# Four levels of a triangular inverse on TensorE: one loop of four passes, or four copies in a row

## The chip, the cores and the metric

The kernel runs on one core of a Trainium2 chip. The metric is device time in microseconds (us), from launch to the last store, for one execution of the whole program. Lower is better.

## The reference

The program computes two transformer-like blocks on 256 tokens of width 1024. The first is a gated linear recurrence, sparse attention and a mixture of 32 experts. The second has a cross attention, a convolution, a bidirectional RWKV-7 recurrence and a feed-forward stage of 16 experts with three weight matrices each. The change lies in the RWKV-7 recurrence of the second block:

```python
def wkv7_scan(r, w, k, v, kk, a, reverse):
    def step(state, inp):
        r_t, w_t, k_t, v_t, kk_t, a_t = inp
        sa = jnp.einsum('bhij,bhj->bhi', state, -kk_t)
        state = (state * w_t[..., None, :]
                 + sa[..., :, None] * (kk_t * a_t)[..., None, :]
                 + v_t[..., :, None] * k_t[..., None, :])
        y_t = jnp.einsum('bhij,bhj->bhi', state, r_t)
        return state, y_t
```

It has 6 heads of width 64 and runs once forward and once in reverse over the 256 tokens. After it come a projection (`w_out`), the router and the experts:

```python
hid = jax.nn.silu(jnp.einsum('becd,edf->becf', xe, w_gate)) * jnp.einsum('becd,edf->becf', xe, w_up)
ye = jnp.einsum('becf,efd->becd', hid, w_down) * gates[..., None].astype(h.dtype)
```

Everything is float32. The expert weights of the second block alone are 16 x 3 x 4 MB.

## The kernel before

All five engines run one instruction stream each. SyncE (`sp`) issues the weight loads, 2 MB each, into rings and free pieces of on-chip memory, in a fixed order, each after a wait on the semaphore that says that its place is free.

The recurrence is done in chunks of 32 tokens. The outer loop over `PAIRS` runs twice and is written out: in pair 0 the forward direction (`d` = 0) works on the first 128 tokens and the reverse direction (`d` = 1) on the second 128, in pair 1 they swap. Each pair has 4 chunks, 6 heads and 2 directions, so nearly every step is 48 small products, with operands of 32 or 64 partitions. `product` (L2317) issues all of them. The compiler makes two weight loads and two matmuls of one such float32 product, so the trace shows 96 matmuls for 48 products. In order, TensorE does for each pair:

- `turned`: transposes of three inputs of each direction;
- `pair_products`: the chunk products of both directions, 96 products in all;
- `bonus`: 48 products, then two waits on `prod_out` (L2477);
- the loop `with pe.Fori(0, 4) as lev` (L2478), a loop that the engine's sequencer runs with registers and a branch. Each pass inverts the unit triangle one level further (blocks of 1 to 2, ... up to 32 rows): `merge_first` (L2363) for both directions, 24 products each of `OM` and `X` into PSUM, then `merge_second` (L2374), 24 products each of `XT` and `PONE`. A pass is thus 96 products, 192 matmuls and 192 weight loads. The waits in it compare a semaphore with `lev * 2 + const` or `lev * 4 + const`, which the sequencer works out in registers;
- `solved`, `reads`: 48 products each, with the inverse;
- `additions`: 192 products, with `strips` put in between. A strip is one product of 128x128 that belongs to the output projection and is on no one's critical path. `STRIPS` says by hand where they go, counted in products from the start of a direction's additions: in pair 0 six at 34 and six at 92 of the first direction, and twelve at 48 of the second; in pair 1 at 27, 85 and 41;
- `advance`: four short sequential steps of the state, each with an answer from ScalarE in between, some strips beside them.

Beside each level the other engines work in turn: VectorE adds the identity to the first product (L3395), ScalarE copies the second (L1402), VectorE transposes that copy (L3399), GpSimd masks the next `OM` (L973). Their four levels are written out already.

In SyncE's order two loads belong to this stretch: one 2 MB piece of `w_e_down` (L709) goes when `lev_full` reaches 1, that is with the first `merge_first` of pair 0, and the next loads of expert weights (L704, four 2 MB pieces to begin with) wait for `y_out` to reach 4, which VectorE gives at the end of pair 1 (L3429). The memory that they fill is in use by the recurrence until then.

Of the kernel before, what the change touches and what calls it, by code (L numbers as in the profile page):

```python
# [137 lines left out]
def build(nc, A, out):  # L138
    with ExitStack() as ctx:
# [5 lines left out]
        def S(name):  # L145
            if name not in sems:
                sems[name] = ctx.enter_context(nc.semaphore(name))
            return sems[name]
# [1336 lines left out]
        def _(pe):  # L1485
# [833 lines left out]
            def turned(p, d):  # L2319

                pe.wait_ge(S("prep_ready"), 4 * p + 2 + d + 1)
                if p:
                    pe.wait_ge(S("y_out"), 2 * p - 1 + d)
                    pe.wait_ge(S("state_out"), 2 * NC4 * p - 1 + d)
                    pe.wait_ge(S("strips_out"), 2 * p - 1 + d)
                for b, src in ((2, KKIN), (3, PEND), (0, KEND)):
                    if not p:
                        is_out(pe, prior[4 * d + b])
                    for c in range(3):
                        ins = nc.tensor.transpose(dbank(d, b, c * P, P), src[d][:, c, :], ident)  # L2330
                    ins.then_inc(S("tok_full"), 1)

            def pair_products(p, d, i):

                if i == 0:
                    if not p:
                        is_out(pe, prior[4 * d + 1])
                    pe.wait_ge(S("tok_out"), 6 * p + 3 * d + 1)
                else:
                    pe.wait_ge(S("tok_out"), 6 * p + 3 * d + 3)  # L2340
                a = (PIN, KIN)[i][d]
                both = front[d][:, 0:1152].rearrange("p (w q) -> p w q", w=3)[:, 0:2 + p:1 + p]
                for pc in range(3):
                    for c in range(NC4):
                        tc = slice(32 * c, 32 * c + 32)
                        for par in range(2):
                            r = slice(64 * par, 64 * par + 64)
                            o = dbank(d, ((1, 2), (0, 3))[i][par], 0, 192)[tc].rearrange("p (w n) -> p w n", w=2)
                            ins = product(o[:, :, 32 * pc:32 * pc + 32], a[r, pc, tc],
                                          both[r, :, P * pc + 32 * c:P * pc + 32 * c + 32])  # L2350
                ins.then_inc(S("prod_full"), 1)

            def bonus(p, d, t):

                pe.wait_ge(S("prod_out"), 8 * p + 2 + 2 * d + 2)
                for h in range(HEADS6):
                    for c in range(NC4):
                        tc = slice(32 * c, 32 * c + 32)
                        ins = product(dbank(d, 0, 64 * h, 64)[tc], block32(BT[d], c, unit(h)),
                                      VTOK[tc, t, 64 * h:64 * h + 64])  # L2360
                ins.then_inc(S("rhs_full"), 1)

            def merge_first(p, d, lev):  # L2363

                pe.wait_ge(S("om_out"), lev * 2 + (14 * p + 4 + d + 1))
                pe.wait_ge(S("x_out"), lev * 2 + (10 * p + d + 1))
                pe.sem_inc(S("level_begun"), 1)
                for u in range(HEADS6):
                    for c in range(NC4):
                        ins = product(dbank(d, 3, 32 * u, 32)[32 * c:32 * c + 32], block32(OM[d], c, u),  # L2370
                                      block32(X[d], c, u))
                ins.then_inc(S("lev_full"), 1)

            def merge_second(p, d, lev):  # L2374

                pe.wait_ge(S("lev_out"), lev * 4 + (16 * p + d + 1))
                pe.sem_inc(S("level_begun"), 1)
                for u in range(HEADS6):
                    for c in range(NC4):
                        ins = product(dbank(d, 3, 192 + 32 * u, 32)[32 * c:32 * c + 32], block32(XT[d], c, u),  # L2380
                                      block32(PONE[d], c, u))
                ins.then_inc(S("lev_full"), 1)

            def solved(p, d):

                pe.wait_ge(S("lev_out"), 16 * p + 14 + d + 1)
                pe.wait_ge(S("solve_out"), 6 * p + d + 1)
                pe.wait_ge(S("prod_out"), 8 * p + 6 + d + 1)
                for i in range(2):
                    for h in range(3 * i, 3 * i + 3):  # L2390
                        for c in range(NC4):
                            tc = slice(32 * c, 32 * c + 32)
                            ins = product(dbank(d, 1 + i, 128 * (h - 3 * i), 128)[tc], block32(XT[d], c, unit(h)),
                                          RHS[d][tc, h, :])
                    ins.then_inc(S("rhs_full"), 1)
# [4 lines left out]
            def reads(p, d):  # L2400

                pe.wait_ge(S("solve_out"), 6 * p + 2 + 2 * d + 2)
                for h in range(HEADS6):
                    for c in range(NC4):
                        tc = slice(32 * c, 32 * c + 32)
                        ins = product(lane(d, c, h, 0, 96), WU[d][tc, h, 0:64], PP[d][tc, h, :])
                ins.then_inc(S("qg_full"), 1)
# [7 lines left out]
            def strip(p, k, s):  # L2415
                product(ps[:, 512 * s:512 * s + P], MIX[:, k, p * P:(p + 1) * P],
                        wout2[s // 4][:, k, s % 4 * P:s % 4 * P + P], False)
# [10 lines left out]
            def additions(p, d, t):  # L2428

                pe.wait_ge(S("rg_out"), 4 * p + 2 * d + 2)  # L2430
                for i in range(2):
                    for h in range(HEADS6):
                        for c in range(NC4):
                            tc, hc = slice(32 * c, 32 * c + 32), slice(64 * h, 64 * h + 64)
                            a, b = (PTOK[d][tc, h, :], WU[d][tc, h, 64:128]) if i == 0 else \
                                (KTOK[d][tc, hc], VTOK[tc, t, hc])
                            strips(p, d, 24 * i + 4 * h + c)
                            ins = product(lane(d, c, h, 192, 64), a, b, i == 0 and h < 2)
                for i in range(2):
                    for h in range(HEADS6):  # L2440
                        for c in range(NC4):
                            tc, hc = slice(32 * c, 32 * c + 32), slice(64 * h, 64 * h + 64)
                            a, b = (WU[d][tc, h, 64:128], PR_[d][tc, h, :]) if i == 0 else \
                                (VTOK[tc, t, hc], block32(KR[d], c, unit(h)))
                            strips(p, d, 48 + 24 * i + 4 * h + c)
                            ins = product(lane(d, c, h, 384, 32), a, b, False)
                if not p:
                    ins.then_inc(S("step_full"), 1)
# [19 lines left out]
            for p, pair in enumerate(PAIRS):  # L2468
                for d, t in pair:
                    turned(p, d)  # L2470
                for i in range(2):
                    for d, t in pair:
                        pair_products(p, d, i)
                for d, t in pair:
                    bonus(p, d, t)
                for d, t in pair:
                    pe.wait_ge(S("prod_out"), 8 * p + 2 + 2 * d + 2)  # L2477
                with pe.Fori(0, 4) as lev:  # L2478
                    for d, t in pair:
                        merge_first(p, d, lev)  # L2480
                    for d, t in pair:
                        merge_second(p, d, lev)
                for d, t in pair:
                    solved(p, d)
                for d, t in pair:
                    reads(p, d)
                for d, t in pair:
                    additions(p, d, t)
                assert not units[p]
                for s in range(-1, NC4):  # L2490
                    for d, t in pair:
                        if s >= 0:
                            advance(p, d, s)
                        for b in STEP_STRIPS.get((p, s, d), ()):
                            strip(p, 3, b)
# [1085 lines left out]
```

## Time and profile before

| | us |
|---|---|
| median of 3 runs | 1618.83 (1616.43 to 1620.4) |
| the profiled execution's own time | 1615.83 |
| its span, first to last instruction | 1614.0 |
| TensorE busy | 1319.3 (82%), mean granted clock 0.91 |
| VectorE, ScalarE, GpSimd busy | 457.7, 284.1, 132.4 |
| DMA | 514 MB, mean 318 GB/s |
| recurrence of the second block | about 1041 to 1135 of the span |

How to read it: the share of the chain of waits is PE 52% and DMA 42%, and the two take turns. In the stages of the experts (530 to 910 and 1200 to 1600 in the span) the DMA engines move 428 GB/s without a gap. In between TensorE leads, and in the recurrence the DMA engines are almost idle (3 to 97 GB/s in these slices of the page). Times of rows are microseconds from the start of the span. [...]

### The profile page before, as it was taken

How to read it: one execution, taken by the hardware profiler on the slowest of the kernel's cores; microseconds unless marked ns; L12 is line 12 of the kernel's file. 1: busy time of each engine (PE TensorE's matmuls, PEld its weight loads, DVE VectorE, ACT ScalarE, POOL GpSimd, SP SyncE). 2: the span in 40 equal slices, each digit the busy share in tenths (PEclk: the TensorE clock that was granted, in tenths of full speed). 3: DMA queues.
4: the chain of work that ended last, by engine and by line, in shares of the span. 5: the costliest groups of instructions: out<-in, count | busy, mean ns of one | idle time of the engine just before them, and what ended most of it. 6: DMA issues, size and time to landing. Idle time of an engine off the chain costs nothing.

```text
span 1614.0 us, 27193 instructions
## 1 busy us (share of the span) xinstructions
PE 1319.3 (82%) x11722; PEld 745.9 (46%) x11722; DVE 457.7 (28%) x968; ACT 284.1 (18%) x634; POOL 132.4 (8%) x289
## 2 busy tenths in 40 slices
PE   5999999999999887787778689988886657666665
PEld 4765887888563332232223278677432212211211
DVE  1346337431463322222222243753510000000001
ACT  0101214650021110111011113332211101101001
POOL 4000013000000000000000004122000000000000
PEclk9999999999999989988999889998998787888878
DMA  9799665133479999999999691310899999999997
GB/s 346 280 389 340 189 235 178 65 108 133 158 277 421 428 427 428 429 428 428 428 428 426 289 339 54 97 56 3 358 426 427 427 428 428 428 428 429 428 427 295
DMA packets 86630, 513.98 MB, mean 318 GB/s; under 512 B 8537, under 2 KB 13066, under 8 KB 61842
## 3 DMA queue, kind: packets, MB, share of 16 engines
q1 hardware_dynamic: 82450, 502.84, 76.7%
q0 software_dynamic: 3424, 9.27, 1.6%
q8 instruction: 66, 1.08, 0.3%
q10 hardware_dynamic: 672, 0.65, 0.1%
q14 instruction: 18, 0.15, 0.0%
HBM read 507.84 MB, written 3.15 MB: 317 GB/s over the span
## 4 chain that ended last, share of the span: by engine, by line
PE 52%; DMA 42%; DVE 2%; issue 1%; ACT 1%; SPq 1%; POOL 0%; DVEq 0%; ACTq 0%
PE ps L1518 42%; DMA arena<-in_w_e_down 19%; DMA ring<-in_exp_w 19%; PE ps L2317 4%; DMA ring<-in_w_e_up 2%; PE ps L1610 2%; DMA ring<-in_w_in 1%; PE ps L2089 1%; PE ps L2567 0%; PE ps L1766 0%; SPq L653 0%; PE ps L1762 0%; PE ps L1565 0%; PE ps L2330 0%; PE ps L2118 0%
## 5 line engine op out<-in xcount | busy, mean ns | idle before, releaser
L1518 PE MATMUL ps<-ring,arena 128*32 128x512 f32 (+4 forms) x1844 | 268.1, 650 | 101.1 <-DMA ring<-in_exp_w 85.3
L1518 PE MATMUL ps<-ring,hTs 128*32 128x512 f32 (+2 forms) x992 | 214.7, 633 | 46.1 <-DMA ring<-in_w_e_up 25.0
L1518 PE MATMUL ps<-hTs,ring 128*128 128x256 f32 (+1 forms) x992 | 215.5, 381 | 0.0
L1518 PEld LDWEIGHTS ps<-ring,arena 128*32 128x32 f32 (+1 forms) x1844 | 81.8, 128 | 267.5 <-issue 178.9
L1518 PEld LDWEIGHTS ps<-hTs,ring 128*128 128x128 f32 (+1 forms) x992 | 182.9, 188 | 29.1 <-issue 4.5
L1518 PE MATMUL ps<-arena,vv 128*32 128x512 f32 (+2 forms) x560 | 92.1, 710 | 84.5 <-DMA arena<-in_w_e_down 78.0
L1518 PEld LDWEIGHTS ps<-ring,hTs 128*32 128x32 f32 (+1 forms) x992 | 76.1, 136 | 155.0 <-issue 106.4
L3142 DVE COPY hTs<-ps 64x512 f32<-64x512 f32 x32 | 22.2, 693 | 259.5 <-PE ps L1518 259.5
L1518 PE MATMUL ps<-arena,hTs 128*32 128x512 f32 x480 | 95.0, 632 | 0.0
L1518 PEld LDWEIGHTS ps<-arena,vv 128*32 128x32 f32 (+2 forms) x560 | 28.1, 142 | 132.4 <-DMA arena<-in_w_e_down 86.3
L1236 ACT COPY arena<-ps 128x512 f32<-128x512 f32 x32 | 18.7, 585 | 387.9 <-PE ps L2067 387.9
L1518 PE MATMUL ps<-arena,ring 128*128 128x256 f32 (+2 forms) x320 | 69.7, 382 | 2.8 <-issue 2.0
L3523 DVE TENSOR_TENSOR vv<-vv,ps 64x512 f32<-64x512 f32 x16 | 11.0, 690 | 212.4 <-ACT vv L1465 212.4
L1518 PEld LDWEIGHTS ps<-arena,ring 128*128 128x128 f32 (+1 forms) x320 | 59.0, 190 | 13.3 <-issue 5.7
L2089 PE MATMUL ps<-arena 64*128 64x512 f32 x256 | 63.0, 610 | 1.6 <-DVE arena L3151 1.6
L3517 DVE TENSOR_TENSOR hTs<-ps,nffn 128x128 f32<-128x128 f32 x32 | 7.8, 285 | 194.8 <-PE ps L1518 194.8
L900 POOL COPY arena<-arena 128x128 f32 (+1 forms) x64 | 16.9, 293 | 437.9 <-PE ps L2067 417.0
L1465 ACT ACTIVATE vv<-ps 64x512 f32<-64x512 f32 x16 | 9.4, 590 | 207.6 <-PE ps L1518 207.6
L1518 PEld LDWEIGHTS ps<-cst,low 64*128 64x128 f32 (+1 forms) x544 | 33.1, 189 | 27.4 <-issue 27.4
L1518 PE MATMUL ps<-arena 128*32 128x512 f32 (+7 forms) x270 | 44.5, 409 | 0.0
L2823 DVE SCALAR_TENSOR_TENSOR arena<-ring,ccol,arena 128x512 f32<-128x512 f32 x56 | 42.1, 752 | 2.0
L1471 ACT COPY hTs<-ps 128x512 f32<-128x512 f32 x16 | 9.4, 585 | 163.1 <-PE ps L1518 163.1
(473 smaller groups left out, 1470.9 us busy)
## 6 DMA issues: line engine op xcount, KB each, us to landing
ring<-in_exp_w SPq DMA_DIRECT2D x91, 2048.0 KB, 21.8
arena<-in_w_e_down SPq DMA_DIRECT2D x28, 2048.0 KB, 25.7
ring<-in_w_e_gate SPq DMA_DIRECT2D x24, 2048.0 KB, 32.1
ring<-in_w_e_up SPq DMA_DIRECT2D x24, 2048.0 KB, 37.7
ring<-in_w_in SPq DMA_DIRECT2D x22, 2048.0 KB, 13.7
ring<-in_ada_w SPq DMA_DIRECT2D x12, 2048.0 KB, 15.9
arena<-in_w_e_up SPq DMA_DIRECT2D x8, 2048.0 KB, 34.7
arena<-in_w_e_gate SPq DMA_DIRECT2D x8, 2048.0 KB, 33.2
```

Of the source, the lines that this page charges most:

```text
L900: ins = nc.gpsimd.tensor_copy(gateR[:, t], mid(gatep1[:, t, cols], 4))
L1236: nc.scalar.copy(HT1, ps[:, m * 512:m * 512 + 512]).then_inc(S("hidT1_ready"), 1)
L1465: nc.scalar.activation(hid2, u[0:64], ACT.Silu).then_inc(S("silu2_ready"), 1)
L1471: nc.scalar.copy(YE, ps[:, 1024:1536]).then_inc(S("ye_ready"), 1)
L1518: return nc.tensor.matmul(o, lhsT, rhs, start=start, stop=stop)
L1610: ins = nc.tensor.matmul(o, wt[:, k, c * P:(c + 1) * P], hT[:, k, :], start=k == 0 and c % 2 == 0, stop=k == KC - 1, skip_group_check=True)
L2089: ins = nc.tensor.matmul(ps[:, b * 512:b * 512 + 512], HT1[r, 256 + t * P:256 + (t + 1) * P], YE1[r, :], start=False, stop=True, skip_grou ...
L2317: return nc.tensor.matmul(o, lhsT, rhs, start=start, stop=True, skip_group_check=True)
L2823: ins = stt(part, wt[:, k, :], ccol[:, k:k + 1], part, ALU.mult, ALU.add)
L3142: cp(part1, u[64:128]).then_inc(S("part_ready"), 1)
L3517: ins = tt(xe[:, ks], v3(ps[:, o:o + P], 4), last(nffn8[:, ks], CAP), ALU.mult)
L3523: tt(hid2, hid2, ps[64:128, (e % 2) * 512:(e % 2) * 512 + 512], ALU.mult).then_inc(S("hid2_ready"), 1)
```

## The change

TensorE's loop over the four levels becomes a loop of Python, so that its body stands four times in the instruction stream. It does so in both pairs. The products, their order and the work of the other engines stay. `lev` is then a number: the waits compare with constants, and the register operations, the compare and the branch are gone.

```diff
@@ -2475,7 +2475,7 @@
                     bonus(p, d, t)
                 for d, t in pair:
                     pe.wait_ge(S("prod_out"), 8 * p + 2 + 2 * d + 2)
-                with pe.Fori(0, 4) as lev:
+                for lev in range(4):
                     for d, t in pair:
                         merge_first(p, d, lev)
                     for d, t in pair:
```

## Rows read from the trace of the kernel before

**Rows 1.** The page, part 3: DMA queue, packets, MB, share of 16 engines.

```profile
q8 instruction: 66, 1.08, 0.3%
```

**Rows 2.** Timeline of TensorE, pair 0: start, length, operation, count, idle before.

```profile
1048.66 0.75 PE L2317 MATMUL ps<-arena,ring 32*32 32x64 f32 x36 [1.22 <-issue]
1049.47 1.20 PE L2317 MATMUL ps<-ring 32*32 32x32 f32 x88
1053.09 1.76 PE L2317 MATMUL ps<-ring 32*32 32x32 f32 x104 [2.42 <-issue]
1055.17 3.05 PE L2317 MATMUL ps<-ring 32*32 32x32 f32 x192 [0.31 <-issue]
1058.52 2.58 PE L2317 MATMUL ps<-ring 32*32 32x32 f32 x192 [0.30 <-issue]
1061.53 2.42 PE L2317 MATMUL ps<-ring 32*32 32x32 f32 x192 [0.43 <-ACT ring L1402]
1064.21 1.51 PE L2317 MATMUL ps<-arena,ring 32*32 32x128 f32 x48 [0.25 <-DVE ring L3399]
...
1069.36 0.72 PE L2317 MATMUL ps<-ring,arena 32*64 32x64 f32 x42 [0.83 <-DVE ring L3406]
```

**Rows 3.** The same timeline for pair 1.

```profile
1095.30 0.87 PE L2317 MATMUL ps<-arena,ring 32*32 32x64 f32 x48 [1.61 <-issue]
1096.26 1.29 PE L2317 MATMUL ps<-ring 32*32 32x32 f32 x76
1098.82 1.94 PE L2317 MATMUL ps<-ring 32*32 32x32 f32 x116 [1.27 <-issue]
1101.13 3.05 PE L2317 MATMUL ps<-ring 32*32 32x32 f32 x192 [0.37 <-ACT ring L1402]
1104.47 2.91 PE L2317 MATMUL ps<-ring 32*32 32x32 f32 x192 [0.29 <-issue]
1107.81 2.42 PE L2317 MATMUL ps<-ring 32*32 32x32 f32 x192 [0.43 <-ACT ring L1402]
1110.46 1.51 PE L2317 MATMUL ps<-arena,ring 32*32 32x128 f32 x48 [0.23 <-DVE ring L3399]
```

**Rows 4.** DMA queues in the window 1065 to 1083, after the loop of pair 0.

```profile
q8 instruction: 6, 0.10, 2.1%
```

**Rows 5.** DMA queues in 1055.1 to 1064.2, passes 2 to 4 of pair 0.

```profile
q8 instruction: 1, 0.02, 0.7%
```

**Rows 6.** DMA queues in 1101.1 to 1110.4, passes 2 to 4 of pair 1; all rows.

```profile
q14 instruction: 1, 0.01, 0.3%
```

**Rows 7.** Line 2478, the loop's own instructions: count, ns min/median/max, first and last start.

```profile
L2478 PEldq FUSED_REGOPS  x8: 50/50/50, 1049.2 to 1107.5; - x8
...
L2478 PEldq COMPARE_BRANCH  x8: 76/220/246, 1054.6 to 1110.1; - x8
```

**Rows 8.** Timeline of SyncE, the weight loads around the stretch.

```profile
1050.18 0.33 SPq L709 DMA_DIRECT2D arena<-in_w_e_down  x1
1135.10 0.33 SPq L704 DMA_DIRECT2D ring<-in_w_e_up  x1
```

**Rows 9.** Waits of SyncE from 1041 to 1170: waiter, releaser, us, times, longest.

```profile
SPq L704 <- DVE arena L3429: 84.5, 1, 84.5
```

**Rows 10.** Busy time by engine in four stretches; then PEclk, DMA share, GB/s.

```profile
1055.10:1058.20 3.10, 3.03 (x192) 2.95 (x192) 1.42 (x4) 0.45 (x2) 1.18 (x2) 0.50 0.57 238
...
1061.50:1064.20 2.70, 2.38 (x192) 2.11 (x192) 1.46 (x4) 0.52 (x2) 2.70 (x3) 1.00 0.00 0
...
1134.50:1170.00 35.50, 28.85 (x116) 14.48 (x116) 20.48 (x53) 8.87 (x15) 3.95 (x4) 0.90 0.97 404
...
1204.00:1590.00 386.00, 252.93 (x1806) 81.65 (x1798) 15.79 (x41) 33.65 (x55) 10.85 (x40) 0.82 1.01 428
```

**Rows 11.** Timeline of TensorE, one group of six strips in pair 0.

```profile
1073.11 1.60 PE L2317 MATMUL ps<-ring,hTs 128*128 128x128 f32 x12
```

**Rows 12.** Chain of waits, its first long DMA piece after the recurrence.

```profile
1204.96 22.54 DMA arena<-in_w_e_down
```

## The prediction

> **What bounds the kernel now.** I read the page first. The chain of waits alternates between TensorE and DMA, so the stage has to be found in which the change lies. It is the recurrence, 1041 to 1135. There SyncE waits 84.5 us for one thing, the last result of pair 1 [rows 9], and issues the next expert weights the moment it has it, at 1135.10 [rows 8]. From then on the DMA engines are full (share 0.97 at 404 GB/s, later 1.01 at 428) [rows 10], and from 1204.96 the chain is mostly DMA [rows 12]. So what the recurrence gains or loses moves the start of a full stream of loads and reaches the end one for one. Nothing absorbs it: the loads that could run early are held back by memory, not by time.
>
> Next I read the timeline of TensorE in this stretch, looking at what stands in the brackets. A pass of the loop is 192 matmuls. Passes 2, 3 and 4 of pair 0 start at 1055.17, 1058.52 and 1061.53, and the code behind the loop at 1064.21 [rows 2]: 3.35, 3.01 and 2.68 us. The short waits between them, 0.25 to 0.43 us, are answers of ScalarE and VectorE or the loop's own instructions. But pass 1 starts at 1049.47 and takes 5.7 us, for it stands still for 2.42 us after 88 matmuls, put down to "issue". In pair 1 pass 1 stops for 1.27 us after 76 matmuls, and a stop of 1.61 us lies just ahead of it, in `bonus` [rows 3]. In the middle of a row of like products no semaphore can be meant.
>
> The queues explain it. Instructions come by DMA, 66 packets and 1.08 MB, so 16.4 KB each [rows 1]. From the restart at 1095.30 to the one at 1098.82 there are 48 + 76 = 124 matmuls and as many weight loads, with 8 or so instructions of the sequencer: 256, or 64 bytes each. At 1048.66 and 1053.09 it is 36 + 88 = 124 again. One packet thus holds 256 instructions, and **TensorE stops at the end of a packet until the next is there**. In code that runs straight the packets follow at 3.52 us (1095.30 to 1098.82), and six of them lie within 18 us, at most 3.6 us apart [rows 4]. In passes 2 to 4 pair 0 has one packet in 9.1 us and pair 1 has none of this queue [rows 5, 6]: these passes run out of instructions that are there already. That is the point of the case. 192 matmuls and 192 loads are 1.5 packets; fetched, they cost 5.3 us, and from the loop 2.7 to 3.35.
>
> **The change part by part.** *Taken away:* in each of two pairs 3 taken branches, their register work and that of the waits. The branch takes 220 ns and the register operation 50 [rows 7]. The idle time ahead of the passes bounds what this can give, 0.29 to 0.43 us at a time, six times: 2.0 us at most if the code were there for nothing. As part of it is an answer of ScalarE, I would take half, but in fetched code it hides behind the fetch, so 0 goes into the sum.
>
> *Added:* three copies of a pass for each pair, 384 instructions and about 4 waits each, 1164; the loop's own in the one pass that stays, some 10, go. 1154 / 256 = 4.5 packets a pair. The price of a packet is the nearest row's, 3.5 us, since these passes are the same products as the ones that were stopped. 4.5 x 3.5 = 15.8 us a pair.
>
> *Replaced:* what TensorE did from the restart in pass 1 to the end of the loop. Pair 0: 1053.09 to 1064.21 is 11.1 us, of which one packet's 3.5 would pass anyway, so 7.6 go. Pair 1: 1098.82 to 1110.46 is 11.6, so 8.1 go. Net: 15.8 - 7.6 = **8.2** and 15.8 - 8.1 = **7.7 us**, together 15.9.
>
> Is the rest of a pass a stronger limit than the fetch? At the lower clock a pass is 3.05 us [rows 2, 10] plus 0.3 us of waiting, that is 2.2 us for each packet's worth. It is under 3.5, so answers and clock both hide behind the fetch inside the levels, and ScalarE, VectorE and GpSimd only wait longer.
>
> *A load beside it:* one 2 MB load goes out at 1050.18 [rows 8], and the restart that should come 3.5 us after 1048.66 comes after 4.43 [rows 2]. That load is still running at 1055 to 1058 (share 0.57) [rows 10], where the changed kernel fetches its second packet. I take the same 0.9 us again. Bounds: 0 and 1.8.
>
> *The strips:* a group of six takes 1.60 us [rows 11] and gives the fetch time. Pair 0 is moved by half a packet (4.5), so the groups stand elsewhere among the packets: the twelve strips of direction 1 fall into a packet with about 52 products of 2 short matmuls (some 12 ns each), 3.2 + 1.2 = 4.4 us, while their neighbours still take 3.5. Against an even spread that is 0.9 to 1.7 us; I take 1.3, bounds 0 and 2. In pair 1 the shift is 9.0 packets in all, so nothing changes there. The wait of 0.83 us for VectorE at 1069.36 [rows 2] now overlaps with a fetch: -0.5, bounds -0.8 and 0.
>
> *The clock:* in the loops the granted clock is at 0.50 for some passes and back at 1.00 in the last one of pair 0 [rows 10]. [...] The dense work of the loop is what stood ahead of the rise before. I take 0, bounds 0 and 4 for both pairs.
>
> Sum: 15.9 + 0.9 + 1.3 - 0.5 = **17.6 us**. On the profiled execution, 1615.83, that is 1633.4. Its own time is 3.0 us under the median of the runs, and on the median it is 1618.8 + 17.6 = **1636.4**.
>
> [...]
>
> **The rivals.**
> *The copies come for nothing (faster).* If the fetch ran on ahead while TensorE waits for ScalarE and VectorE in each level, only the loop's own cost would go: six times about 0.3 us, 1618.8 - 1.9 = 1616.9. It decides from the point at which a packet comes in less than the 2.0 us that its share of a pass takes. For it: before the stops there is always work without answers to wait for. Against it: six packets in 18 us also hold in `additions` and `advance`, where answers are waited for. [...]
>
> *The fetch is hidden in part.* If waiting time lets the next packet be asked for early, a packet would cost about 2.6 us instead of 3.5: 9 x 0.9 = 8.1 less, 1628. Same evidence against it.
>
> *The stops feed on each other.* The clock stays at the lower level after both pairs (+4) and each packet costs what the one at 1053.09 did for half of them (+0.9 x 4): 1644.
>
> *It doesn't do what it says:* none of weight; both forms issue the same products.
>
> **How the numbers follow.** Forecast, the sum within its bounds: 0.78. Low end: 15.9 - 0.8 with a packet at 3.45 (9 x 0.05 less) and the second restart not late, 14.6, so 1633; high end: 15.9 + 1.8 + 2 + 4 = 23.7, so 1642.5. Stops that feed on each other: 0.08. Hidden in part: 0.08. For nothing: 0.06. To leave no more than 2 in 10 out I reach on the low side toward the partly hidden case and on the high side to the third rival: 1630 to 1644. A measurement of this kernel can tell about 0.3%, 4.9 us, from no change. Slower by more: 0.78 + 0.08 + 0.08 = 0.94 less a little, 0.93. Same: 0.05. Faster: 0.02, since the fast rival's 1.9 us lies within the 0.3%.
>
> **What would show it.** The changed trace should have about 75 packets in q8 instead of 66, nine of them where the levels run. Each level should take 5 to 5.7 us on TensorE with stops of 1 to 2 us at "issue" in the middle of its products, 128 matmuls apart at most. The first expert load should leave at about 1152.7 instead of 1135.10, and the DMA stage after it should be as long as before. Wrong would be: levels of 3 us; no more packets in q8; packets closer than 3 us; or a later stage that gives the time back.

## The result, and the profile after

| | us |
|---|---|
| before, median of 4 runs | 1618.68 (1616.43 to 1620.40) |
| after, median of 4 runs | 1643.85 (1640.88 to 1647.38) |
| ratio after to before | 1.0159, 95% interval 1.0145 to 1.0172 |
| the profiled execution of after | 1646.21, span 1644.4 |

The four levels written out are slower, by 25.2 us where 17.6 were forecast. The interval of the ratio is 23.5 to 27.8 us. The time lies at the very end of the stated range, 0.15 us inside it, and with the ratio taken on the median that was known then just outside it (1618.83 x 1.0159 = 1644.6). It is beyond the 1642.5 that the sum's own bounds allowed. Medians and ratios here leave out one disturbed run (`e7_load_in_steps`, 2171.9 us at a granted clock of 0.55).

The page of the changed kernel has nine more packets in "q8 instruction" than [rows 1], as counted ahead, and "q14 instruction" has 18 on both pages. Only TensorE's code differs, so q8 is the queue that brings it its instructions (packets, MB, share):

```profile
q8 instruction: 75, 1.23, 0.3%
```

The timeline of TensorE in pair 0, the rows that wait for "issue" and the first row of the additions, answers to [rows 2] (start, length, operation, count, idle before; where the bracket has "issue", the trace names no engine and no line that TensorE waited for):

```profile
1049.37 0.95 PE L2317 MATMUL ps<-arena,ring 32*32 32x64 f32 x34 [1.77 <-issue]
...
1053.65 2.06 PE L2317 MATMUL ps<-ring 32*32 32x32 f32 x126 [2.05 <-issue]
1059.76 2.07 PE L2317 MATMUL ps<-ring 32*32 32x32 f32 x127 [4.04 <-issue]
1063.75 1.99 PE L2317 MATMUL ps<-ring 32*32 32x32 f32 x127 [1.92 <-issue]
1067.83 2.08 PE L2317 MATMUL ps<-ring 32*32 32x32 f32 x126 [2.09 <-issue]
1071.74 2.13 PE L2317 MATMUL ps<-ring 32*32 32x32 f32 x127 [1.83 <-issue]
1075.46 0.80 PE L2317 MATMUL ps<-ring 32*32 32x32 f32 x42 [1.59 <-issue]
...
1083.30 0.72 PE L2317 MATMUL ps<-ring,arena 32*64 32x64 f32 x42 [0.85 <-DVE ring L3406]
```

The levels no longer show. What shows is the packet: 126 or 127 matmuls in 2.0 us, then 1.6 to 2.1 us of nothing. From one restart to the next it is 3.7 to 4.1 us, with one of 6.1. TensorE's matmuls are busy for 12.68 of 26.20 us (1050.00 to 1076.20). Narrow windows of the DMA queues show where the time goes: behind the load, the packets of pair 0's levels start at 1061.0, 1065.1, 1069.3 and 1072.9, which is 1.2 to 1.5 us behind a restart each time, and the next restart is 2.4 to 2.8 us later still. The 2.0 us of work are over before that. Pair 1 has the same picture, six such stretches from 1113.02 to 1136.31. Its first row and the start of what is behind it answer to [rows 3] and to the end of the recurrence in [rows 8]:

```profile
1103.27 1.17 PE L2330 MATMUL ps<-cst,arena 128*128 128x128 f32 x9 [1.00 <-ACT arena L1430]
...
1132.14 1.98 PE L2317 MATMUL ps<-ring 32*32 32x32 f32 x121 [1.63 <-issue]
1136.31 2.55 PE L2317 MATMUL ps<-arena,ring 32*32 32x128 f32 x41 [1.49 <-issue]
```

```profile
1163.07 0.33 SPq L704 DMA_DIRECT2D ring<-in_w_e_up  x1
```

The first expert load leaves at 1163.07 instead of 1135.10, where 1152.7 was forecast. The DMA stage behind it keeps its length: from its first long DMA piece in the chain of waits to the end of the span it is 409.0 us in both (1204.96 to 1614.0, 1235.42 to 1644.4). Between that load and that piece lie 2.5 us more than before, which single executions also show without a change: from the first expert load to the end it is 478.9 and 483.1 us in two executions of the kernel before, and 481.3 and 482.1 us in two of the changed one.

All comparisons below use two stretches of the profiled executions, in the same way for each kernel. Pair 0 goes from TensorE's first transpose (L2330) of pair 0 to that of pair 1. Pair 1 goes from there to SyncE's first expert load (L704).

| kernel | q8 packets | pair 0 | pair 1 | run against before |
|---|---|---|---|---|
| before | 66 | 47.6 | 46.9 | |
| before, again (`e11_loops_again`) | 66 | 48.2 | 46.0 | 1.0004 |
| after | 75 | 62.2 | 59.8 | 1.0159 |
| after, again (`e0_copies`) | 75 | 62.3 | 59.7 | 1.0158 |
| `e1_pair1` | 71 | 47.6 | 57.9 | 1.0056 |
| `e2_pair0` | 71 | 61.7 | 49.1 | 1.0091 |
| `e4_two_by_two` | 69 | 55.9 | 53.1 | 1.0067 |
| `e3_late_load` | 75 | 60.5 | 59.2 | 1.0156 |
| `e7_load_in_steps` | 75 | 60.0 | 58.3 | 1.0129 |
| `e5_fill` | 76 | 63.3 | 59.2 | 1.0182 |
| `e8_loop_load_pass2` | 66 | 49.1 | 47.0 | 0.9995 |
| `e9_half_packet` | 67 | 53.1 | 49.9 | 1.0034 |
| `e10_whole_packet` | 67 | 53.8 | 46.8 | 1.0054 |

### The profile page after: what moved, and what is told of

The parts are those of the page before. It is cut to its first block, busy times and chain, and to the rows that moved or that the text cites. A ratio compares the mean times of both kernels' runs of the same rounds, so it can differ in the third digit from the quotient of the medians.

```text
span 1644.4 us, 27127 instructions
## 1 busy us (share of the span) xinstructions
PE 1336.0 (81%) x11722; PEld 756.7 (46%) x11722; DVE 457.6 (28%) x968; ACT 284.5 (17%) x634; POOL 132.5 (8%) x289
## 4 chain that ended last, share of the span: by engine, by line
PE 52%; DMA 41%; issue 3%; DVE 2%; ACT 1%; SPq 1%; POOL 0%; DVEq 0%; ACTq 0%
PE ps L1518 41%; DMA arena<-in_w_e_down 19%; DMA ring<-in_exp_w 19%; PE ps L2317 5%; DMA ring<-in_w_e_up 2%; PE ps L1610 2%; DMA ring<-in_w_in 1%; PE ps L2089 1%; PE ps L1766 0%; SPq L653 0%; PE ps L1762 0%; DVE stats L2726 0%; PE ps L1565 0%; PE ps L2330 0%; PE ps L1821 0%
## 5 line engine op out<-in xcount | busy, mean ns | idle before, releaser
L2317 PE MATMUL ps<-ring 32*32 32x32 f32 (+2 forms) x1824 | 33.6, 241 | 26.4 <-issue 26.3
L1518 PE MATMUL ps<-arena 128*32 128x512 f32 (+7 forms) x270 | 46.8, 419 | 0.0
L2317 PEld LDWEIGHTS ps<-ring 32*32 32x32 f32 (+1 forms) x1824 | 30.4, 142 | 28.6 <-issue 28.2
```

The source lines that it names most:

```text
L1518: return nc.tensor.matmul(o, lhsT, rhs, start=start, stop=stop)
L2317: return nc.tensor.matmul(o, lhsT, rhs, start=start, stop=True, skip_group_check=True)
```

## The experiments

**One pair at a time.** The theory is that fetched code is the cost. The rival is that the two written-out stretches spoil each other.

```diff
-                with pe.Fori(0, 4) as lev:
+                if p == 0:                       # e1_pair1: pair 0 keeps the loop; e2_pair0: the other way round
+                    with pe.Fori(0, 4) as lev:
...
+                else:
+                    for lev in range(4):
```

> Only pair 1 is written out, pair 0 keeps its loop. Theory (fetched code is the cost, pair by pair, and the 2 MB load beside pair 0 adds to pair 0 alone): TensorE in pair 1 as in the changed kernel, about 13 us longer from the transposes of pair 1 to its additions; q8 has 70 or 71 packets; 4.5 packets x 3.9 - 8.1 = 9.5 and 2 us for solved and reads at the lower clock: the run is 11 to 13 us over before, 1630 to 1632. Rival (the cost comes from the two written-out stretches acting on each other, through the clock or the position of the strips): pair 1 alone costs 8 us or less, 1627.

> Only pair 0 is written out. Theory: 13.8 us as in the changed kernel, of which 2.6 are the packet that waits for the 2 MB load, and half a packet of shift for pair 1: 1632 to 1634; q8 has 70 or 71 packets. Rival (acting on each other): 8 us or less, 1627. If the sum of this run's and the other run's cost is 25 to 28 us, the parts add up.

The medians were 1629.62 and 1634.30 beside 1619.54 for before: 10.1 and 14.8 us, 24.8 together. That is the whole within the noise, so the parts add up, and so do the stretches (11.0 and 16.3 against 27.5). The rival's 8 us is out for pair 0 by the time of the run (11.5 to 18.1 us). For pair 1 the run's interval, 5.8 to 12.1 us, still holds it, and it is the stretch that decides: 57.9 against 46.9 us. `e1_pair1` came out a little under its range and `e2_pair0` a little over it. In `e2_pair0` pair 0 costs 14.1 us, and pair 1, which still has its loop, costs 2.2 us more than before. That second number had no place in the prediction.

**Fewer copies.** Two passes with two levels in each.

```diff
-                with pe.Fori(0, 4) as lev:
-                    for d, t in pair:
-                        merge_first(p, d, lev)
-                    for d, t in pair:
-                        merge_second(p, d, lev)
+                with pe.Fori(0, 2) as two:
+                    for one in range(2):
+                        for d, t in pair:
+                            merge_first(p, d, two, one)
+                        for d, t in pair:
+                            merge_second(p, d, two, one)
```

> A loop of two passes with two levels in each: 1.5 packets of new code a pair instead of 4.5. Theory (what counts is the number of packets): q8 has 69 packets, the second level takes 5.5 to 6 us, the third and fourth 3 us each; a pair costs 1.5 x 3.9 less one pass of 3.1, about 2.8 us, and 2 more in pair 0 for the load: 6 to 8 us over before, 1625 to 1627. Rival (what counts is that branches are gone, or the copies in themselves): half of the branches stay, so half of the cost, 12 us, 1631.

It has 69 packets, as expected, but took 1631.11: 11.6 us, the rival's number and not the theory's 6 to 8. The timeline of TensorE says why, first in pair 0, then in pair 1:

```profile
1052.27 2.19 PE L2317 MATMUL ps<-ring 32*32 32x32 f32 x125 [2.42 <-issue]
1058.57 2.07 PE L2317 MATMUL ps<-ring 32*32 32x32 f32 x124 [4.11 <-issue]
1062.69 0.86 PE L2317 MATMUL ps<-ring 32*32 32x32 f32 x47 [2.05 <-issue]
1063.86 5.71 PE L2317 MATMUL ps<-ring 32*32 32x32 f32 x384 [0.31 <-issue]
```

```profile
1108.20 2.27 PE L2317 MATMUL ps<-ring 32*32 32x32 f32 x124 [1.92 <-issue]
1112.08 2.06 PE L2317 MATMUL ps<-ring 32*32 32x32 f32 x126 [1.62 <-issue]
1116.39 6.16 PE L2317 MATMUL ps<-ring 32*32 32x32 f32 x384 [2.25 <-issue]
```

The second pass, 384 matmuls, runs in one piece in 5.7 and 6.2 us, 2.9 and 3.1 us a level, just as the theory wanted. So the branches are not what costs. From the first transpose to the end of the levels the two pairs take 6.8 and 5.1 us more than before, and there the average of 1.5 packets misleads: TensorE stops a whole number of times, three in the first pass of pair 0. In pair 1 the record of the compare-and-branch stands at 1115.80, 2.0 us after the end of the last instruction ahead of it, which is one of the loop's own too. So it seems that the closing branch lies just behind a packet's boundary, and that pass 2 waits for a packet of which it needs one or two instructions. In pair 0 the load takes its 2 us again (4.11). The other 1.5 and 1.1 us stand behind the levels; in pair 0 there are stops of 0.48 and 0.61 us in the additions that before did not have.

**The 2 MB load.** Between the restarts at 1053.65 and 1059.76 of the changed kernel, the DMA queues show the load and one packet of instructions. From 1055.8 to 1057.4 it is the load alone, and from 1057 to 1058, where the load ends, the packet is there:

```profile
q1 hardware_dynamic: 43, 0.70, 102.6%
```

```profile
q1 hardware_dynamic: 27, 0.34, 80.5%
q8 instruction: 1, 0.02, 6.2%
```

The packet starts at 1057.4, 3.8 us behind the restart instead of 1.2 to 1.5. Two runs move this load in the changed kernel: first behind the levels of pair 0, then into the sequential steps of pair 0.

```diff
             sp.wait_ge(S("conv_centred"), 2)
-            sp.wait_ge(S("lev_full"), 1)
+            sp.wait_ge(S("lev_full"), 16)       # e3_late_load
+            sp.wait_ge(S("state_out"), 3)       # e7_load_in_steps, in place of the line above
             down_tile(0, 1)
```

> The changed kernel, but the 2 MB load of w_e_down that went with the first product of pair 0's levels waits for the end of these levels. Theory (the second packet of pair 0's levels lay behind this load in its DMA engine until it was through): the restart that came after 6.1 us comes after 3.9, and the first one after 3.9 instead of 4.3: 2.2 to 2.6 us less than the changed kernel, 1641. Rival (the long interval is the sequencer's, held in a semaphore wait): it stays at 6 us and nothing changes, 1644.

> The changed kernel, with the 2 MB load of w_e_down sent after the third answer of pair 0's steps, where TensorE needs few instructions. Theory (a packet asked for while the load runs waits for the load's end, and costs that only where TensorE needs it at once): no interval over 4.4 us in pair 0's levels and no new stop in the additions; 2 to 2.6 us less than the changed kernel, 1641.5. Rival (the long interval has another cause, and turns up at any place): no gain, 1644.

In `e3_late_load` the restart intervals in the levels are 3.6 to 4.0 us and the one of 6.1 is gone, which rules out the rival. But no gain shows in the time of the run (1645.24, ratio 1.0136 to 1.0175; the stretches of the one profiled execution are 2.3 us shorter together). The load now meets another packet, which comes between 1080 and 1081, at the load's end, and there is a new stop in the additions of pair 0:

```profile
1080.68 0.44 PE L2317 MATMUL ps<-ring,arena 32*64 32x64 f32 x19 [0.85 <-DVE ring L3406]
1082.89 0.42 PE L2317 MATMUL ps<-ring,arena 32*64 32x64 f32 x23 [1.77 <-issue]
```

`e7_load_in_steps` sends it at 1095.24, where TensorE waits for ScalarE anyway:

```profile
1054.40 2.06 PE L2317 MATMUL ps<-ring 32*32 32x32 f32 x126 [2.42 <-issue]
1058.31 2.07 PE L2317 MATMUL ps<-ring 32*32 32x32 f32 x127 [1.85 <-issue]
1061.76 1.99 PE L2317 MATMUL ps<-ring 32*32 32x32 f32 x127 [1.37 <-issue]
```

Pair 0 is 2.3 us shorter than in the two executions of the changed kernel, as expected, and pair 1 1.4 us. No interval in the levels is over 4.1 us; a stop of 0.58 us in the additions is new. The median of three runs is 1639.47 beside 1644.73, but the intervals of the two ratios overlap (1.0095 to 1.0163, 1.0128 to 1.0188), so the time of the run agrees with the expectation and does not prove it. What the traces show is that a packet which would have come during the 2 MB load comes as the load ends (1057.4 in the changed kernel, 1080 to 1081 in `e3_late_load`), and that the long stop moves with the load and is gone where TensorE waits anyway.

The same was tried on the kernel before:

```diff
-            sp.wait_ge(S("lev_full"), 1)
+            sp.wait_ge(S("lev_full"), 5)
```

> The kernel before, with its loops, and the 2 MB load sent when the second pass of pair 0's loop begins instead of the first. Theory: the packet of pass 1 does not share its DMA engine with the load and comes after 3.5 us instead of 4.4; the next packet is asked for after the loop, when the load is through; 0.9 us less in the stretch, 1 us or less in the run, which 3 rounds can't tell from none. Rival (the next packet is asked for within the loop and would wait for the load past the loop's end): a stop behind the loop, 1 to 2 us more.

It gives nothing (0.9995, interval 0.998 to 1.001). Its restart in pass 1 comes after 4.16 us (1049.34 to 1053.50) with no load beside it, against 4.43 [rows 2]. In the kernel before, that packet starts at 1050.4, ahead of the load's first data at 1051.1. So the 0.9 us that the prediction read from that row as the load's price was mostly not the load's. No stop follows right behind the loop, so the rival did not come true as stated; but pair 0 of the profiled execution is 0.9 to 1.5 us longer than in the two executions of before, nearly all of it behind the levels, and the cause of that is open.

**The clock.** The changed kernel with dense work in the stops.

```diff
+            def warm(d):
+
+                product(dbank(d, 1, 0, 256), ident, cst[:, 0:256])
...
                 ins.then_inc(S("lev_full"), 1)
+                if lev:                          # without the condition in merge_second
+                    warm(d)
```

> The changed kernel once more, beside the next three, on the same chip: 1641 to 1647, 23 to 27 us over before.

> The changed kernel with a product of 128 x 256 on constants after each half of a level (15 for each direction less one, 14 a pair in all), written to a bank that is free there and overwritten later: 4 more instructions each, 0.2 packets a pair, and about 0.75 us of dense work each, which lies in the stops. Theory (the stops let the clock fall, and the clock costs 2 us a pair in solved and reads and some of the 3.9 against 3.5 us a packet): the clock is at 1.00 for most of the levels, solved and reads take 5.2 to 5.6 us instead of 7, and the run is 1 to 4 us under the changed kernel in spite of the added work. Rival A (the packet's interval does not hang on the clock): intervals stay at 3.8 to 3.9, only solved and reads get shorter. Rival B (the clock has no part): the run is 1 us or more over the changed kernel.

The granted clock and the busy times, changed kernel (levels of pair 0, then `solved` and `reads` of pair 0), and below it the filled kernel (second half of the levels of pair 0). The columns are the stretch, its length, busy time of PE, PEld, DVE, ACT and POOL, PEclk, DMA share and GB/s:

```profile
1050.00:1076.20 26.20, 12.68 (x786) 11.89 (x780) 5.42 (x15) 2.71 (x8) 8.21 (x9) 0.50 0.23 84
1076.20:1083.30 7.10, 6.25 (x200) 5.86 (x189) 1.85 (x4) 4.04 (x7) 0.00 (x0) 0.71 0.02 5
```

```profile
1062.50:1073.50 11.00, 9.94 (x401) 6.64 (x400) 2.72 (x8) 1.28 (x4) 5.86 (x5) 1.00 0.02 4
```

In pair 0 of the changed kernel the granted clock is 0.50 for all of the levels, and still 0.50 when `solved` begins (1076.20 to 1078.90). With the fill it is 0.50 from 1050.00 to 1062.50 and 1.00 from there to 1083.36. The first products of `solved` in the changed kernel and in the filled one:

```profile
1076.12 2.75 PE L2317 MATMUL ps<-arena,ring 32*32 32x128 f32 x46
```

```profile
1073.50 1.51 PE L2317 MATMUL ps<-arena,ring 32*32 32x128 f32 x48
```

So the clock's part is real: 2.75 against 1.51 us for the first half of `solved`, and 7.3 us from there to the additions where before had 5.15 [rows 2]. In pair 1 alone (`e1_pair1`) it is 7.4 against 5.5, and with the fill 5.3. Rival A holds for the packets: with the fill, at a granted clock of 1.00, TensorE restarts 3.7 to 4.2 us apart in pair 0 (1071.39, 1075.63, 1079.36, 1083.36) and 3.9 in pair 1 (1124.40, 1128.31, 1132.20). But the run is not faster: 1647.50 beside 1644.73, with intervals that overlap. In pair 0 the filled levels take 2.3 us more from the restart in the first level to `solved`, and `solved` and `reads` 1.4 us less. So the added work takes what the clock gives back. That fits rival B's number without its reason, and as a cure the fill fails.

**The position of the packets.** The 2.2 us of pair 1 in `e2_pair0` was tested on the kernel before, with its loops, by adding code to pair 0 only.

```diff
                 pe.wait_ge(S("rg_out"), 4 * p + 2 * d + 2)
+                if (p, d) == (0, 1):
+                    for _ in range(32):          # e10_whole_packet: 64
+                        product(dbank(d, 3, 480, 32)[0:32], ident[0:32, 0:32], ident[0:32, 0:32], False)
```

> The kernel before, with its loops, and 32 narrow products (128 instructions, half a packet) added ahead of the additions of direction 1 in pair 0, into columns that nothing uses. Theory (what pair 0 does to the packet boundaries costs pair 1 too, since stops fall elsewhere and the strips stand away from them; 2.2 us where only pair 0 was written out): from the first transpose of pair 1 to the first expert load 48.5 to 49.5 us instead of 46.9. Rival (that 2.2 us was chance between executions): 46.5 to 47.3. Pair 0 itself: 1.5 to 2.5 us more.

> The same with 64 narrow products, a whole packet. Theory: pair 1 finds its boundaries where they were, 46.5 to 47.5 us; pair 0 is one packet longer, 3.5 to 4 us. Rival (any added code costs pair 1): 48.5 or more.

> The kernel before once more, for a second profiled execution: 47.6 and 46.9 us for the two pairs, each within 0.5, if single executions can be compared to that.

The stretch of pair 1 ends with these loads of SyncE and begins with these transposes, half a packet first, whole packet second:

```profile
1094.84 1.17 PE L2330 MATMUL ps<-cst,arena 128*128 128x128 f32 x9 [1.00 <-ACT arena L1430]
...
1144.78 0.33 SPq L704 DMA_DIRECT2D ring<-in_w_e_up  x1
```

```profile
1095.74 1.17 PE L2330 MATMUL ps<-cst,arena 128*128 128x128 f32 x9 [1.00 <-ACT arena L1430]
...
1142.53 0.33 SPq L704 DMA_DIRECT2D ring<-in_w_e_up  x1
```

Half a packet of shift costs pair 1 3.1 us (49.9 us against 46.8), a whole packet nothing, though it is twice as much code. Two executions of the unchanged kernel lie 0.9 us apart in pair 1 (46.9, 46.0) and 0.6 in pair 0, both outside the 0.5 us that was expected. The stops fit: in the middle of products of pair 1 they add up to 5.7 us with half a packet, and to 3.6 with a whole one. So the traces show that the position of the boundaries matters, with one profiled execution each. The times of the runs do not separate the two: medians 1625.59 and 1625.68, over before by 1.1 to 9.9 and 5.5 to 12.0 us.

Missed: pair 0 grew by 5.5 and 6.2 us, where 1.5 to 2.5 and 3.5 to 4 were expected. The timelines show most of it. The added products took 2.2 and 4.2 us, stops added 1.2 and 0.5, and the twelve strips of direction 1 behind them took 4.44 and 3.72 us where before had 2.94, at a granted clock of 0.63 and 0.65.

## Why the prediction was right or wrong

**Right: the bound, the mechanism and the sign.** The recurrence reaches the end one for one within the spread of single executions, the packets are 256 instructions, nine more are needed, and the levels run at the pace of their arrival. The fetch was not hidden: TensorE stood still for 1.6 to 2.1 us behind every 126 or 127 matmuls (4.0 behind the load). Nor was the branch the cost: in `e4_two_by_two` the pass behind it ran in one piece, 384 matmuls in 5.7 and 6.2 us.

**Wrong: the sizes.** The steps that failed are the price of a packet, taken from one row (3.5 us, measured 3.86), and two terms put at nothing, the clock behind the levels (measured 4.0 us) and the position of the packets in pair 1 (about 2); the load was taken too small as well. The two pairs together took 27.5 us more in each of two profiled executions (122.0 against 94.5), where the sum had 17.6. By its own terms:

- *Price of a packet.* I took 3.5 us, the nearest pair of restarts. In the levels of the changed kernel it is 3.86 (1109.26 to 1136.31, seven packets), and 3.9 in pair 0 away from the load. In the prediction's formula a pair has 5.5 packets at this price, 4.5 added and the one that "would pass anyway". Eleven times 0.36: +4.0 us. The row of before that showed 4.43 was set aside as the load's; `e8_loop_load_pass2` gave 4.16 without a load. The price should have been a mean over rows, and its upper end in the range.
- *The load.* 0.9 taken, 2.3 measured: +1.4. Before had the same wait: in its own passes 2 to 4 only one packet came [rows 5], and it started at 1057.0, behind the load. The loop hid it. I read that row as proof that the loop needs none, and did not ask when the packet had been asked for.
- *The clock behind the levels.* 0 taken with bounds 0 and 4; 2.1 us in pair 0 and 1.9 in pair 1. I argued from the rise in the last pass of the loop [rows 10], but that rise followed dense passes (TensorE busy for 3.03 of 3.10 us), which are just what the change removes (12.68 of 26.20 us). The bound of 4 was my estimate, and no row or run shows where it comes from; what the runs show in its place is a granted clock of 0.50 in the levels of pair 0, and 7.3 us instead of 5.15 for `solved` and `reads` behind them. The bound was right and the choice in it wrong.
- *Pair 1's position.* "In pair 1 the shift is 9.0 packets in all, so nothing changes there" holds behind the levels of pair 1 only. Ahead of them it has the half packet of pair 0: 2.2 us in `e2_pair0` (and 59.8 against the 57.9 of `e1_pair1`, 1.9).
- *The strips.* 1.3 taken; from the additions of pair 0 to the transposes of pair 1 it is 19.97 against 18.87 us, 1.1. The wait for VectorE that was to overlap with a fetch is still 0.85 us: +0.5.

17.6 + 4.0 + 1.4 + 4.0 + 2.2 - 0.2 + 0.5 = 29.5, which is 2.0 more than the stretch shows. The rows put 1.1 of that into the levels of pair 0, which with what stands ahead of them took 11.4 us more (1041.07 to 1076.03 against 1040.64 to 1064.21), where the terms give 8.2 + 0.9 + 2.0 + 1.4 = 12.5. The formula charges the half packet at the end in full proportion, 1.9 us, but the products of the levels in it took 0.57 us (1075.46 to 1076.03): in these levels TensorE stopped behind whole packets only, 126 or 127 matmuls each. The other 0.9 us lie in pair 1, where single executions of one kernel differ by as much, and no run here divides them.

The medians differ by 25.2 and 25.4 us and the stretch by 27.5. The interval of the ratio reaches to 27.8 us, so this is no contradiction. The profiled executions of the changed kernel are in the upper half of its runs (1646.21 and 1645.79, the lowest 1640.88), and what a run at 1641 does otherwise was not profiled.

Of the rivals, the one in which the stops feed on each other came nearest (1644), and its clock part came true. That its number fits so well is luck: its price for a packet (half of them at 4.4) did not occur, and the load and the position, which did cost time, are not in it. No version tried beats the kernel before.

## What to carry to other kernels

A stretch of narrow matmuls can be bound by the arrival of its instructions: look for idle time put down to "issue" in the middle of equal instructions, count the instructions between two restarts, and price new code by that. Here a packet of 256 mostly took 3.5 to 4.2 us and its narrow products 2, so the loops whose body was already there beat every form with copies that was tried. Count packets whole, and ask of each where its boundary falls (half a packet of shift cost the next stage 3.1 us here), which load it queues behind (2.3 us) and what the stops do to the clock of the code behind them (4.0 us for the two pairs together).

## What the runs showed of the hardware that was not expected

- A packet of instructions due during a 2 MB load came only as the load ended: 6.1 us between restarts instead of 3.9, on and off with the load's place (`e3_late_load`, `e7_load_in_steps`).
- A loop stood still for 2.0 us at its closing branch although the next pass was there already and then ran in one piece, 384 matmuls in 6.16 us (`e4_two_by_two`, pair 1). That a packet's boundary lies there is argued from the count of instructions.
- Half a packet of extra code in one stage cost the next stage 3.1 us, and a whole packet cost it nothing, in one profiled execution each.
- The pace of the packets did not follow TensorE's clock: restarts 3.6 to 4.2 us apart at a granted clock of 0.50 (pair 1 of the changed kernel, 1116.77 to 1136.31), and 3.7 to 4.2 us at 1.00 (the filled kernel, 1071.39 to 1083.36 in pair 0 and 1124.40 to 1132.20 in pair 1).
